# Output projection: the last weight sum of its last step made by two accumulating transfers from GpSimd's queue

## The reference

```python
mixed = g_na * (y_na @ w_branch_na[l]) + g_ml * (y_ml @ w_branch_ml[l])
x = layer_norm(DEEPNORM_ALPHA * x + mixed @ w_out[l], ln1_g[l], ln1_b[l])
f = conv_glu(x, ffn_w_up[l], ffn_conv_w[l], ffn_conv_b[l], ffn_w_down[l])
x = layer_norm(DEEPNORM_ALPHA * x + f, ln2_g[l], ln2_b[l])
```

## Time and profile before

| | |
|---|---|
| median of 3 runs | 2666.44 us (2666.24 to 2668.01) |
| the profiled execution's own time | 2666.18 us |
| its span | 2664.6 us |
| TensorE busy | 2645.0 us, 99% |
| TensorE weight load busy | 2257.3 us, 85% |
| VectorE busy | 2107.3 us, 79% |
| ScalarE busy | 1401.5 us, 53% |
| GpSimd busy | 313.7 us, 12% |

### The profile page before, as it was taken

How to read it: one execution, slowest core, us unless ns; L and a number is a source line. 1 busy time by engine, 2 the same in 40 slices (tenths; PEclk the granted TensorE clock), 3 DMA queues, 4 the chain that set the end, 5 groups by cost and what they waited for, 6 DMA issues and landing times.

```text
span 2664.6 us, 36972 instructions
## 1 busy us (share of the span) xinstructions
PE 2645.0 (99%) x13859; PEld 2257.3 (85%) x13859; DVE 2107.3 (79%) x2725; ACT 1401.5 (53%) x1912; POOL 313.7 (12%) x383
## 2 busy tenths in 40 slices
PE   8999999999999999999999999999999999999998
PEld 7888888888888888888888888888888888888887
DVE  5655647676878777558899999999999988888888
ACT  4544444444655556324457666666666665444444
POOL 2000011111000000011111111111111101000003
PEclk9999999999999999999999999999999999999999
DMA  5333334335776775689627777877777778655633
GB/s 167 95 91 99 95 96 103 100 97 116 187 174 151 168 164 164 216 275 363 223 89 171 201 198 183 222 196 183 210 199 188 188 192 313 243 188 211 246 127 111
DMA packets 516612, 466.32 MB, mean 175 GB/s; under 512 B 16232, under 2 KB 456348, under 8 KB 512096
## 3 DMA queue, kind: packets, MB, share of 16 engines
q1 hardware_dynamic: 418448, 311.79, 37.9%
q0 software_dynamic: 94400, 147.36, 22.6%
q10 hardware_dynamic: 3600, 4.98, 0.5%
HBM read 383.83 MB, written 78.69 MB: 174 GB/s over the span
## 4 chain that ended last, share of the span: by engine, by line
PE 96%; DVE 2%; DMA 0%; ACT 0%; POOL 0%; issue 0%; POOLq 0%; ACTq 0%; DVEq 0%; SPq 0%
PE ps L2914 20%; PE ps L2916 10%; PE ps L2546 10%; PE ps L2548 10%; PE ps L2547 10%; PE ps L2783 9%; PE ps L2837 6%; PE ps L2836 6%; PE ps L2838 6%; PE ps L2784 5%; PE ps L2540 1%; PE ps L2763 1%; PE ps L2742 0%; DVE aop L2242 0%; PE ps L2872 0%; DVE dw L2082 0%
## 5 line engine op out<-in xcount | busy, mean ns | idle before, releaser
L2914 PE MATMUL ps<-aop,uw 128*128 128x512 f32 x2336 | 585.4, 393 | 1.6 <-ACT uw L1366 0.8
L2914 PEld LDWEIGHTS ps<-aop,uw 128*128 128x128 f32 x2336 | 420.4, 189 | 76.7 <-ACT uw L1366 1.0
L2082 DVE TENSOR_TENSOR uw<-quad,uw 128x1024 fp32r<-128x1024 f32 x292 | 356.8, 1222 | 46.7 <-ACT uw L1366 45.5
L1618 DVE TENSOR_TENSOR wlo<-raw,whi 128x512 fp32r<-128x512 f32 x256 | 175.5, 689 | 270.3 <-ACT whi L1019 266.1
L1019 ACT ACTIVATE whi<-raw 128x512 fp32r<-128x512 f32 x256 | 159.8, 629 | 406.2 <-PE ps L2548 400.6
L1366 ACT ACTIVATE uw<-quad 128x1024 fp32r<-128x1024 f32 x292 | 308.5, 1056 | 78.2 <-PE ps L2916 71.9
L2916 PEld LDWEIGHTS ps<-aop,uw 128*128 128x128 f32 x2336 | 318.8, 191 | 22.7
L2916 PE MATMUL ps<-aop,uw 128*128 128x256 f32 x2336 | 326.0, 283 | 0.0
L2546 PE MATMUL ps<-x_hl,whi 128*128 128x512 f32 x768 | 304.8, 397 | 1.0 <-DVE wlo L1618 1.0
L2548 PE MATMUL ps<-x_hl,wlo 128*128 128x512 f32 x768 | 300.4, 391 | 0.0
L2547 PE MATMUL ps<-x_hl,whi 128*128 128x512 f32 x768 | 300.1, 391 | 0.0
(11 more groups left out here) (360 smaller groups left out, 4687.1 us busy)
## 6 DMA issues: line engine op xcount, KB each, us to landing
quad<-in_ffn_w_up SPq DMA_DIRECT2D x172, 512.0 KB, 3.8
raw<-in_w_in SPq DMA_DIRECT2D x192, 256.0 KB, 2.8
region<-in_ffn_w_down SPq DMA_DIRECT2D x32, 1280.0 KB, 9.1
gq<-in_w_in SPq DMA_DIRECT2D x79, 512.0 KB, 3.9
a_dram<-ah SPq DMA_DIRECT2D x20, 1792.0 KB, 9.1
aopb<-a_dram POOLq DMA_DIRECT2D x28, 1280.0 KB, 8.3
quad<-in_ffn_w_up POOLq DMA_DIRECT2D x42, 512.0 KB, 6.8
w_region<-in_w_out SPq DMA_DIRECT2D x16, 1024.0 KB, 8.5
```

The costliest lines, as they stand in the source:

```text
L1618: nc.vector.tensor_tensor(wlo[:, k % HL, :], raw[:, k % RAW, :], whi[:, k % HL, :].bitcast(F32), ALU.subtract).then_inc(w_lo_ready, 1)
L2082: nc.vector.tensor_tensor(w[:, 1, :, :], src, w[:, 0, :, :].bitcast(F32), ALU.subtract).then_inc(s["op_lo"], 1)
L2914: return mm(ps[:, bank, :], w[:, 0, k, :], a.rearrange("p h t -> p (h t)"), start=i < 2 and k == 0, stop=False, skip_group_check=True)
```

## The change

In the last step (`W_STEPS` - 1) the fourth sum, q12 += q21, is no longer made by VectorE. GpSimd's queue gets two transfers with `accum_op=ALU.add`, one for each piece (128 x 2 x 512, 512 KB), that read q21 once more from w_out in HBM and add it to q12 in SBUF. Ahead of the first stands a wait for the low half of product 2, piece 1 (the last reader of q12 after sum 1), and ahead of each a wait for its piece of the third sum (which reads q12). They count `t1_in[0]` and `t1_in[1]`; ScalarE's two high halves of product 6 wait for these instead of `t_formed`. The other edits renumber: `t_formed` has two counts fewer (`T_W`), the two `t1_in` semaphores start the up-projection 16 higher (`t1_count`).

```diff
--- before.py
+++ after.py
@@ -109,7 +109,7 @@
 C_U = W_STEPS - 1
 N_UP = N_U + 7 * FB
 N_C = C_U + FB
-T_W = 8 * W_STEPS
+T_W = 8 * W_STEPS - 2
 T_U = T_W - 3
 T_UP = T_U + 3 * FB
 H_BANK = (2, 3, 5, 6, 7)
@@ -432,7 +432,7 @@
 
 
         def t1_count(step):
-            return quad_count(step) - (0 if step % 2 else 16)
+            return quad_count(step) + (16 if step % 2 else 0)
 
         def quad_count(step):
 
@@ -897,6 +897,19 @@
             for i, o in enumerate(OPS):
                 pool.wait_ge(s["op_used"], w_piece(1, i, 1) + 1)
                 w_op(1, o)
+
+            def lower_left(step):
+                g, half = step // 2, step % 2
+                src = w_out[0][2 * W_PAIRS * g * P:2 * W_PAIRS * (g + 1) * P, half * 1024:half * 1024 + 512]
+                return src.rearrange("(k b p) c -> p b k c", p=P, b=2)[:, 1, :, :]
+
+            last = W_STEPS - 1
+            pool.wait_ge(s["op_lo"], w_piece(last, 2, 1) + 1)
+            for pc in range(2):
+                first, size = W_PIECES[pc]
+                pool.wait_ge(s["t_formed"], 8 * last + 4 + pc + 1)
+                pool.dma_start(w_region[W_REGIONS[last][1]][:, first:first + size, :], lower_left(last)[:, first:first + size, :],
+                               accum_op=ALU.add).then_inc(t1_in[pc], 16)
 
             for q in range(4):
                 pool.wait_ge(s["first_hi"], FROM["first_hi"] + q + 1)
@@ -1325,6 +1338,8 @@
                     dst = dw[:, n % 3, 0, :, :]
                     if i in (0, 3, 5):
                         act.wait_ge(w_quad_in[r], 16 * w_uses(step, r))
+                    elif step == W_STEPS - 1 and i == 6:
+                        act.wait_ge(t1_in[pc], 16 * (GS // 2 + 1))
                     else:
                         act.wait_ge(s["t_formed"], 8 * step + 2 * {1: 0, 2: 1, 4: 2, 6: 3}[i] + pc + 1)
                 elif n < N_UP:
@@ -2174,7 +2189,7 @@
                         elif i == 5:
                             u2_w(step)
                         operand_lo(w_piece(step, i, pc))
-                        if i in (0, 1, 3, 5):
+                        if i in (0, 1, 3) or i == 5 and step < last:
                             w_form(step, (0, 1, 3, 5).index(i), pc)
                         if step == 0 and pc == 1 and i == 0:
                             mix(KB - 1)
```

## The result

The changed kernel takes 2670.91 us in the median of 15 runs (2669.48 to 2672.80), the kernel before 2666.20 us in the median of 15 beside it (2664.46 to 2668.01): a ratio of 1.0018, 95% interval 1.0011 to 1.0025, or 4.7 us more. The forecast was 2669.1 us with a range to 2670.9.

The account below looks back on a forecast made before the run. TensorE was taken to bound the step, VectorE about 5% behind. A 2.9 us delay less the old 0.22 gave +2.7 on the profiled 2666.18, 2668.9; adjusted towards the runs' median, the forecast was 2669.1 us, range 2666.0 to 2670.9.

Parts of the forecast that it names:

- Removed sums: Last step: without VectorE's two sums, TensorE starts product 6, piece 0 (6.0) with no wait, a gain of 0.22 us.
- Transfers free: Last step: the two accumulating transfers cost nothing, landing in time with 1.3 us to spare at the worst.
- The lock: Last step: GpSimd's two moved subtractions shut out VectorE's operations with two SBUF inputs, making TensorE 2.9 us late.
- The second subtraction is let in when that low half is read: At product 4: VectorE's low half of piece 0 goes between both subtractions; TensorE 1.2 us late at 4.0, 2.9 at 4.1.
- a bound, 3.2 us: At product 4, piece 0: second subtraction straight behind the first, one hold of 4.5 us, 3.4 us late, +3.2 in all.
- The clock: Rival: TensorE's idling in the last step lets its clock fall once, 1.4 to 1.7 us more, 2670.7 us; chance 0.08.
- A late, harmless start: Rival: GpSimd's configuration instruction delays the subtractions until VectorE has caught up; 2666.2 us, chance 0.19 shared with relief alone.
- Nothing takes it back later: After the last step: spins start when TensorE does and the chain beyond moves as a whole, leaving the +2.7 us.

Follow-up runs that it names:

- subtractions first: Changed kernel with GpSimd's first two subtractions put back ahead of the two transfers; 2665.04 us, ratio 0.9998 to the kernel before.
- no fourth sum: Changed kernel without the two transfers, the fourth sum left out, GpSimd's first two subtractions back in step 2; stretch 152.35 us against 152.70 before.
- idle time filled: Changed kernel plus 13 matmuls of unused result before TensorE's wait for product 4, piece 0; 2667.94 us, ratio 1.0011 to the kernel before.
- one subtraction behind: Changed kernel with one of the two subtractions moved ahead of the transfers, one left behind; stretch 153.62 us against 152.70 before.
- VectorE let in: Changed kernel, second subtraction also waiting until VectorE made the low half of product 4, piece 0; stretch 155.40 us against 152.70 before.
- subtractions last: Changed kernel with all four subtractions waiting for the last low half of the last step; 2665.81 us, ratio 1.0003 to the kernel before.
- memsets: Changed kernel with four GpSimd memsets in place of the two subtractions, all four subtractions after the last low half; stretch 152.33 us against 152.70 before.
- the run without transfers: Kernel before with the first two subtractions made to wait for the last step's third sum; 2668.24 us, ratio 1.0012 to the kernel before.

## Why the prediction was wrong

The direction was right, the size was not: 2.7 us forecast, 4.7 measured, a hundredth of a microsecond beyond the range's end.

- **Removed sums: right, a bit undersized.** Forecast was a gain of 0.22 us, measured 0.37 and 0.35 (subtractions first; no fourth sum). I had counted the late start of 6.0 but not what a restart costs, 0.11 us: after the gap the second matmul came 0.34 us behind the first (1373.46 to 1373.80) instead of 0.227, here and after each wait behind which the clock stayed up (idle time filled, one subtraction behind, VectorE let in).
- **Transfers free: right.** They cost nothing (152.33 against 152.35), landed 6.2 us after issue at the latest, and took 1.21 us to issue, between the bounds of 0.72 and 1.54.
- **The lock: right.** The rule of the Trainium skill (SBUF — State Buffer, "Who interferes with whom") held in each run: VectorE rows of 4.93, 4.99, 3.42, 2.56 and 2.63 us beside GpSimd's subtractions, 1.22 beside memsets, as it states that an instruction that only writes doesn't contend.
- **"The second subtraction is let in when that low half is read": this step failed.** I had VectorE and GpSimd alternate. In the change GpSimd's second subtraction followed its first directly though VectorE had been waiting since 1362.73, and held it until 1366.44. The runs showed in its place one hold over both, 3.71 us. In the one row of before GpSimd had a single subtraction, so nothing in it spoke for alternation. Nor is the opposite a rule: between the third and fourth of four subtractions VectorE got its turn (subtractions last, memsets). Those cases differ in the operation that waited (128 x 2 instead of 128 x 1024) and in how far GpSimd's rows overlap (0.04 us instead of 0.52), and no run separates the two; what decides the turn stays open. The other course stood in the prediction as a bound, 3.2 us; measured 3.30. That both sums come out so close is in part luck: counted from the projection's first matmul, the first subtraction's row began 0.5 us earlier than forecast (the issue took 1.21 us, not 1.54) and was 0.5 us longer (2.88 instead of 2.39), which cancels. With the second subtraction made to wait for the low half of 4.0, the kernel costs the 2.70 us of the sum.
- **The clock: a rival that happened, once.** It had 0.08 for one fall, at 1.4 to 1.7 us; measured 1.38. It was priced on top of 2.7, though it is tied to the same failed step: one wait of 3.33 us (and one of 1.82 in the run without transfers) was followed by a fall, two waits of 1.03 and 1.45 us 3 us apart were not, nor one of 0.96. The argument against it also had a slip: the two forecast waits span 1362.34 to 1368.0, 5.7 us and not 4.5, so that TensorE would have worked 48% of that time and not 60%. So the two errors came together, and 3.3 + 1.4 = 4.7 is what the bound and that rival add up to. The range should have contained their sum.
- **A late, harmless start (part of the 0.19): its premise was wrong.** The time of GpSimd's configuration instruction could be read: 0.04 us in the kernel before, 0.50 in the change, where the first subtraction's row starts at 1361.39.

```profile
L905 POOLq MODIFY_POOL_CONFIG  x2: 42/42/42, 1303.8 to 1303.8; - x2
```

```profile
L918 POOLq MODIFY_POOL_CONFIG  x2: 502/502/502, 1361.3 to 1361.3; - x2
```

- **Nothing takes it back later: right.** From first spin to first transpose it is 6.80 us before and 6.81 after, to `uw` 44.41 in both.

## What to carry to other kernels

A transfer put at the head of a queue delays whatever stands behind it; ask where that work lands, and what it meets there. GpSimd's subtractions were free beside ScalarE, TensorE and the one-input or PSUM-reading operations of VectorE (four of them in 9.49 us, stretch 152.34), and held VectorE's operations with two SBUF inputs for up to their full length. Price several in a row as one hold and as two: both were seen. When a wait of some microseconds is forecast for TensorE, price the clock's fall with it, not as a separate mishap. And relief of an engine that isn't the bound shows only once the padding behind it (here the spins) is cut to fit.

## What was not expected of the hardware

- A waiting VectorE operation can be held through two GpSimd subtractions that stand directly behind each other (4.93 and 4.99 us rows in two kernels), and can also be let in between two (1.71 and 1.78 us rows in two others). What decides it is open.
- A VectorE operation on 128 x 2 elements with two SBUF inputs was held 1.5 us as well (1.71 instead of 0.18): its small size didn't protect it.
- GpSimd's first subtraction behind the transfers took 2.88 us with one subtraction there, and two took 5.18, against 2.39 and 4.77 elsewhere: about 0.4 to 0.5 us more directly behind a transfer. Its configuration instruction stands between them, but isn't needed for it: the first memset behind the transfers took 1.43 us instead of 0.96 with no configuration ahead of it. In each case the row begins before the transfer's own row ends (1357.75 against 1357.01 + 1.20 = 1358.21 for the memset), so that the excess may be time in which the issue still runs; this was not tried.
- TensorE's restart cost 0.11 us over the wait itself in each wait with the clock up (0.34 instead of 0.227 us to the second matmul).
- A wait of 1.82 us was followed by a fall of the clock as the one of 3.33 us was, and the fall behind the shorter one lasted longer (eight steps of 0.42 us against six).
